# Hyena stage: the weight chunk of the folded product is split into its parts ahead of the filter's last four tiles instead of behind them

## What is computed

```python
def hyena_filters(L, w1, b1, w2, b2, w3, freq):
    ...
    h = jnp.sin(freq[0].astype(f32) * (z @ w1.astype(f32) + b1.astype(f32)))
    h = jnp.sin(freq[1].astype(f32) * (h @ w2.astype(f32) + b2.astype(f32)))
    h = (h @ w3.astype(f32)).reshape(L, 2, HY_ORDER, HY_W)
    ...
    h = h * jnp.exp(-t * deltas)[:, None, None, :]
    ...
    return jnp.fft.rfft(k2, axis=0)

def hyena_mixer(u, short_w, kf, bias):
    u = dwconv3(u, short_w)
    v, x1, x2 = jnp.split(u, 3, axis=-1)
    z = x1 * long_conv(v, kf[:, 0], bias[0])
    return x2 * long_conv(z, kf[:, 1], bias[1])
```

## Time and profile before

| | us |
|---|---|
| median of 3 runs | 1859.94 |
| lowest, highest run | 1857.67, 1862.53 |
| the profiled execution's own time | 1856.39 |
| its span | 1854.5 |

### The profile page before, as it was taken

One profiled execution on the slowest core, in us unless ns is written; L12 is line 12 of the kernel. 1 busy time (PEld: TensorE's weight loads), 2 busy tenths in 40 slices (PEclk: granted clock), 3 DMA queues, 4 the chain that ended last, 5 costly groups with the idle time before them and its releaser, 6 DMA issues.

```text
span 1854.5 us, 24893 instructions
## 1 busy us (share of the span) xinstructions
PE 1778.2 (96%) x9921; PEld 1477.0 (80%) x9921; DVE 1160.8 (63%) x1846; ACT 805.8 (43%) x1392; POOL 332.2 (18%) x283
## 2 busy tenths in 40 slices
PE   7999999999999998989999999899979999999998
PEld 5778877789998877778888888797756689999887
DVE  6778855588885366356777732566356469888322
ACT  5433344444454444344344432445357545555321
POOL 2014501021101040151111110320000022332100
PEclk9999999999999999999999999899979899999999
DMA  5222322236544431222322233141221154775521
GB/s 194 86 85 91 103 92 80 69 97 182 150 128 169 145 91 46 62 75 80 102 96 98 80 105 100 57 137 57 88 68 33 39 165 121 194 188 143 181 91 58
DMA packets 62356, 195.97 MB, mean 106 GB/s; under 512 B 7386, under 2 KB 10074, under 8 KB 62112
## 3 DMA queue, kind: packets, MB, share of 16 engines
q1 hardware_dynamic: 48960, 162.51, 27.2%
q0 software_dynamic: 12704, 31.34, 7.5%
q10 hardware_dynamic: 576, 0.52, 0.1%
HBM read 188.05 MB, written 6.29 MB: 105 GB/s over the span
## 4 chain that ended last, share of the span: by engine, by line
PE 84%; DVE 7%; issue 4%; ACT 4%; POOL 2%; DMA 0%; SPq 0%; DVEq 0%; POOLq 0%; ACTq 0%
PE ps L405 26%; PE ps L407 25%; PE ps L406 25%; PE ps L410 3%; PE ps L3382 2%; POOL sums L453 1%; ACT ws_h L333 1%; PE ps L3399 1%; DVE ws_l L341 1%; POOL x L1856 1%; DMA x<-in_x 0%; ACT P L3508 0%; DVE tmp L851 0%; PE ps L1106 0%; PE ps L3394 0%
## 5 line engine op out<-in xcount | busy, mean ns | idle before, releaser
L341 DVE TENSOR_TENSOR ws_l<-raw,ws_h 128x1024 fp32r<-128x1024 f32 x228 | 315.9, 1392 | 339.4 <-ACT ws_h L333 339.0
L405 PE MATMUL ps<-h_h,ws_h 128*128 128x512 f32 (+2 forms) x1140 | 446.7, 392 | 19.7 <-DVE h_l L584 9.9
L406 PE MATMUL ps<-h_l,ws_h 128*128 128x512 f32 (+2 forms) x1140 | 435.0, 382 | 0.0
L407 PE MATMUL ps<-h_h,ws_l 128*128 128x512 f32 (+2 forms) x1140 | 434.5, 381 | 0.0
L333 ACT ACTIVATE ws_h<-raw 128x1024 fp32r<-128x1024 f32 x228 | 238.8, 1053 | 284.5 <-PE ps L407 280.0
L405 PEld LDWEIGHTS ps<-h_h,ws_h 128*128 128x128 f32 x1140 | 217.6, 191 | 75.4 <-issue 15.0
L407 PEld LDWEIGHTS ps<-h_h,ws_l 128*128 128x128 f32 x1140 | 217.9, 191 | 43.1
L406 PEld LDWEIGHTS ps<-h_l,ws_h 128*128 128x128 f32 x1140 | 218.8, 192 | 39.1
L405 PE MATMUL ps<-fb_h,ws_h 128*128 128x256 f32 x476 | 133.8, 281 | 0.0
L407 PE MATMUL ps<-fb_h,ws_l 128*128 128x256 f32 x476 | 133.8, 281 | 0.0
L406 PE MATMUL ps<-fb_l,ws_h 128*128 128x256 f32 x476 | 133.1, 280 | 0.0
(11 more groups left out here) (536 smaller groups left out, 3502.0 us busy)
## 6 DMA issues: line engine op xcount, KB each, us to landing
raw<-in_ffn_up SPq DMA_DIRECT2D x88, 512.0 KB, 3.6
raw<-in_w_merge SPq DMA_DIRECT2D x36, 512.0 KB, 4.3
raw<-in_ffn_down SPq DMA_DIRECT2D x22, 512.0 KB, 3.5
raw<-in_w_down SPq DMA_DIRECT2D x22, 512.0 KB, 3.6
raw<-in_w_hy SPq DMA_DIRECT2D x12, 512.0 KB, 3.9
raw<-in_w_sc SPq DMA_DIRECT2D x12, 512.0 KB, 3.5
s<-in_ffn_up SPq DMA_DIRECT2D x17, 256.0 KB, 4.1
s<-in_ffn_up POOLq DMA_DIRECT2D x17, 256.0 KB, 5.1
```

The costliest lines, as they stand in the source:

```text
L341: dve.e.tensor_tensor(w.lo, raw[n % NRAW][:], w.hi, ALU.subtract).then_inc(*lo_made.says(("lo", n)))
L405: pe.e.matmul(o, a.hi, b.hi, start=start, stop=False, skip_group_check=True)
L406: pe.e.matmul(o, a.hi, b.lo, start=False, stop=False, skip_group_check=True)
L407: return pe.e.matmul(o, a.lo, b.hi, start=False, stop=stop, skip_group_check=True)
```

## The change

Two calls are added: ScalarE's and VectorE's lists split up to two chunks further than are in use, at the step ("s", o, 2, 0) of both orders, before the work that belongs to that step.

```diff
@@ hyena_act @@
         def begun(t):
+            if t[0] == "s" and t[2:] == (2, 0):
+                split_hi(used["act"] + 2)
             if t == ("hy", 1):
@@ hyena_dve @@
         def begun(t):
+            if t[0] == "s" and t[2:] == (2, 0):
+                split_lo(used["dve"] + 2)
             if t == ("hy", 1):
```

## The result

The changed kernel takes 1865.84 us in the median of 10 runs, from 1861.38 to 1866.73; the kernel before, run beside it, 1859.47 us, from 1855.74 to 1862.53. The ratio is 1.0030 with a 95% interval of 1.0019 to 1.0041: 0.3% slower. The interval excludes no change; by a bound of 2% it would still count as the same. The forecast was 1866.0, with a range of 1861.2 to 1869.0. The profiled execution took 1861.38 us (span 1859.6), the fastest of the ten, against 1856.39 us (span 1854.5) before.

The account below looks back on a forecast made before the run. TensorE, busy 96% of the span, was taken as the bound, with VectorE's list setting the end of F. Order and clock terms, 1.4 + 1.8 + 1.1 + 1.9 = 6.2 us on 1859.94, gave 1866.1, predicted as 1866; range 1861.2 to 1869.

Parts of the forecast that it names:

- The end of F is set by VectorE's list: F(0,0) and F(1,0) end when VectorE reaches the last filter tile; without any delay F(0,0) could gain 0.3 us.
- First place, order: Chunk 8's split: VectorE stands still 1.11 us more, so F(0,0) ends 0.8 to 1.4 us later; 1.4 expected.
- Second place, order: Chunk 14's split: VectorE stands still 1.77 us behind ScalarE's high part, so TensorE is 1.8 us later in F(1,0).
- The clock: Waits inside F(0,0) and F(1,0) leave TensorE at half clock on the work behind: 1.1 and 1.9 us more.
- Sum: Both places, order and clock together: 1.4 + 1.8 + 1.1 + 1.9 = 6.2 us slower.
- Rival 1: Clock holds or its low stretch is hidden; only VectorE's order counts at both places: 2.6 us slower, 1862.5; chance 0.30.
- Rival 2: The start of F(0,0) and F(1,0) counts, so the earlier chunk gains 9.3 us, 1850.6; chance 0.05.
- The chances: Whole kernel: 0.50 slower (from 1865.5 us), 0.46 within 0.3% of no change, 0.04 faster.

Follow-up runs that it names:

- filled_before: Kernel before plus 15 extra matmuls ahead of F(0,0) and 6 ahead of F(1,0), where TensorE waits; ratio 0.9989 against the kernel before.
- no_stall: Changed kernel with the early split's ScalarE part one step later and VectorE's part two steps later; ratio 1.0016 against the kernel before.
- hold_fixed: As no_stall, but next chunks split behind the last filter tile's low part, and F(1,1)'s chunk at step zT(0); ratio 0.9957 against the kernel before.
- first_place: Kernel before with only chunk 8's split moved early, the second place as before; ratio 1.0005 against the kernel before.
- second_place: Kernel before with only chunk 14's split moved early, the first place as before; ratio 1.0013 against the kernel before.
- filled_after: Changed kernel plus 38 extra matmuls where TensorE waits inside F(0,0) and F(1,0); ratio 1.0005 against the kernel before.

## Why the prediction was right, point by point

- *The end of F is set by VectorE's list.* Right: filled_before won 0.22 us where 0.3 were read from the rows, no_stall started F(0,0) 3.5 us earlier with the tile where it was and won nothing, and hold_fixed, which moved that tile forward, got the 4.0 us of the first place.
- *First place, order: 0.8 to 1.4 us.* hy7 started 1.56 us later, at half clock as expected. The two waits inside F(0,0) ended at 73.18 and 76.64 by the old count, where 73.15 and 76.62 stood in the prediction; what it had too small is the end behind them, since the first matmul behind a wait takes 0.59 us and not 0.43 at half clock (77.43 to 78.02). With the clock held the order's own part of both places is 2.68 us, predicted 2.6. VectorE's added wait was 1.05 us instead of 1.11.
- *Second place, order: 1.8 us.* 1.80 us at the point of the last `mg_l`, with a wait of 1.72 us on VectorE instead of 1.77.
- *The clock: 1.1 + 1.9 us.* Behind hy7's start the shift grew from 1.56 to 2.67 us, 1.1; behind the last product's start at the second place, from 4.47 to 6.57 us, 2.1. The bounds had gone from nothing to 4.6. With the part inside F(0,0), 0.6 us, this is about the 3.9 us that the fillers took away. That half clock would fall on hy7 and on the transposes was read rightly; that the sizes came within 0.2 us is partly luck. The prediction chose 1.1 between two counts, 0.5 and 2.0 us, and 1.9 between 1.6 and 2.6, and neither count is what happened: the clock came back at about 81.4, which is 80.6 by the old count and not 79.0 or 82.4. Where the order is the same, other executions paid otherwise: first_place starts hy7 at 22.87 us of the stretch, as the change does at 22.88, but F(0,1) at 29.89 and not 29.58, so 1.4 us; and second_place paid 1.8 us at the second place instead of 2.1. The Trainium skill says that the same kernel meets the change of clock at different points from run to run (TensorE: Matmul & The Clock Gate, "The HAM clock gate (the "warmup" mystery)"). These differences of 0.3 us agree, as far as different kernels with the same order at one place can show it.
- *Sum: 6.2 us.* 6.57 in the stretch and 6.4 between the medians. Up to 663.02 nothing downstream made it good, and the medians say the same of the whole.
- *Rival 1 (the clock holds), 2.6 us.* It did not hold; filled_after is that case made by hand, and came to 2.68 us.
- *Rival 2 (F's start decides), 9.3 us faster.* F's start did move forward, by 4.0 us at the first place and by 2.0 us at the second beside hy9's end, and gave nothing. The size of the prize was real, though: hold_fixed took 7.0 us with the filter tiles' low parts made earlier.
- *The chances* put half on slower by over 0.3%. The interval of the ratio, 0.19% to 0.41%, lies on both sides of that bound. It excludes no change, though: ten executions told more than the 0.3% that the prediction allowed them.

What a reader could not have told from the profile before is how the clock would answer. The rows gave a fall after waits of 2.66 us and more, and none after 2.0; here it fell behind 2.23 and behind 2.52 us, with three and six matmuls after the wait.

## What to carry to other kernels

A wait at the front of a step is worth what the step's end gives back: look for the last operand that the step needs, on whichever engine makes it, before pricing the wait for the first. Where two engines follow each other in fixed order, moving both halves of a piece of work to the same place can buy a wait (here 1.05 and 1.72 us); the first half may go early alone, and the second belongs where its input is ready and nothing that decides is queued behind it. And a wait that is cut into pieces and moved towards dense work can cost more by the clock than by its length.

## What the runs showed of the hardware

The half clock was more than half of the change's price (3.9 of 6.57 us), although the kernel before has some 6 us of half clock at the same place at a price of 0.2 us: what it slows decides the price, and its length alone doesn't tell it. The filler matmuls kept the granted clock at 1.00, and filled_after lies within 0.1 us of the expected 2.6, so no cost of theirs is seen. In no_stall waits of 0.70 and 1.80 us, with six matmuls between them, were followed by half clock at the second place (the 16 transposes of zT took 3.26 us there and 1.82 before), where 1.87 and 0.64 us, with 21 matmuls between them, were not the earlier trace rows. The executions of one and the same kernel spread over 5 to 11 us, while the stretch agreed to 0.01 us between two kernels that are the same up to the second place, and to 0.3 us for the same order followed by half clock; a fraction of a per cent is seen better there than in the whole time.
